# An attention encoder on one core: the count of branches in the dilated heads applied after the exponential

## The chip, the core and the metric

The kernel runs on one core of a Trainium2 chip. The metric is the device time of one execution in microseconds. An engine is named as the profile names it: PE is TensorE, DVE is VectorE, ACT is ScalarE, POOL is GpSimd, SP the queue that issues the DMAs.

## What is computed

Two sequences (a prompt of 1024 tokens and a sample of 512) go through two layers of width 1024. The first layer has 8 dilated heads ("a") and 8 latent heads ("b") side by side, the second 16 grouped-query heads ("c"). Each layer projects, attends, multiplies with a gate, projects back and normalises. Only the dilated heads matter here. Each is attention over three branches, (window 128, dilation 1), (512, 4), (2048, 16), whose denominators are merged:

```
for window, dilation in ((128, 1), (512, 4), (2048, 16)):      # one branch each
    s = q.k - slope * |t_query - t_key|     where the pair lies in the window and on the dilation, else -1e30
    m = max(s);  p = exp(s - m);  z = sum(p);  o = p.v
w = exp(m_branch - max over branches of m)
out = sum(o * w) / sum(z * w)
```

A pair of query and key may lie in one, two or three of the branches. It has the same score in each, so the result is one softmax in which the exponential of such a pair counts once, twice or three times.

## The kernel before

Everything is feature-major in SBUF; matmuls run on fp32r operands, and a product of better precision is made of parts: hi times hi and lo, and lo times hi.

The attention of a layer is one loop over `G` = heads x 10 tiles of keys (`NS` = 10 slots a head, s = g % 10). Even and odd tokens are kept apart (two "sides"). For a dilated head, slots 0 and 1 each hold two key tiles of the sample, slots 2 to 9 one key tile of the prompt (side 0, then side 1; tile m = 0 to 3). A key tile of 128 meets all 512 (sample: 256) queries of its own side and the 160 or 192 near ones of the other, so a tile is 832 columns wide in slots 0 and 1, 672 for m = 0 and 3, and 704 for m = 1 and 2.

Each engine walks the same slots in order and hands over by semaphores; nothing is planned at run time.

- PE, in slot g: `scores(g)`, then `pv(g - 3)` (LAG = 3), in which one or more `max_unit`s of head h + 1 stand between the part that needs the rounded probabilities and the part that needs their low part, then the remaining max units. `scores` writes the two banks SA, of which there is one copy: it waits for `e_done` of the slot before. The max units write the two halves of SM in turn: unit u waits until DVE is done with unit u - 2. Slots 0 to 3 have three units, slots 4 to 9 two; the heads of kinds b and c have two in each slot.
- `pair_scores` makes one tile for a dilated head out of seven matmuls: three parts for own-side columns (L1917 hi keys; L1918 identity x bias `Bhi`; L1921 low keys with the maximum subtracted), with L1920 adding the low part of the bias, `Blo`, over the 256 or 384 columns near the diagonal, and then three for the near columns of the other side (L1923, L1925, L1927).
- ACT, in slot g: waits for `s_ready`, exponential `PF` <- SA (L2185), then the rounded copy `PH` <- `PF` (L2188), except in slots 3 and 5 (`SLOW_HI`), where DVE makes it (L2380). After it, in slot 3, the inversion of the last head's denominators (`invert`, L2132 and L2134: logarithm and exponential), and in slot 5 that of its own sample.
- POOL, in slot g: the low part `PL` = `PF` - `PH` (L2486), except in slots 4 and 8 (`SLOW_LO`), where DVE makes it one slot later (L2301).
- DVE, in slot g, in this order: `augment` (slot 1, L2291), `normalise` of the last head (slot 4, L2333, waits for the inversion), the low part of slot g - 1 where it is DVE's, the rounded copy where it is DVE's, the first half of the maxima (L2264: adds the bias table to the scores in SM and takes the row maximum), `normalise` of the sample (slot 6), `bias_full` (slot 4), the other maxima, `augment` (slot 7), half of a bias table each in slots 7 and 8 (`bias`, L2245).

The bias of a pair is slope x distance plus the logarithm of the number of branches that hold it, -1e30 where none does. The table `Bhi` (1280 columns a head) is rounded to fp32r. `bias_full` (DVE, L2251) makes the same in full precision for 384 columns, and `bias_low` (POOL, L2468) the difference, `Blo`.

Of the kernel before, what the change touches and what calls it, by code (L numbers as in the profile page):

```python
# [25 lines left out]
BOWN, BCROSS, BLOW = 896, 192, 384  # L26
# [1415 lines left out]
def layer(nc, ar, l, tag, A, S, heads, gpost, ones, epst, xin, xout, sc, base, banks, place, project):  # L1442
# [86 lines left out]
    if NA:  # L1529
        b_hi, b_sum, b_lo = ar.sem(f"a_b_hi"), ar.sem(f"a_b_sum"), ar.sem(f"a_b_lo")  # L1530
# [52 lines left out]
    if NA:  # L1583
        sizes = (512, 4 * BW, 4 * BW, 32, 4 * BLOW, 4096, 4 * BW, 4 * BW, 4 * BLOW, 4 * BLOW)
        offsets = list(itertools.accumulate(sizes, initial=half1))
        BD, BL_ = (at(n, [P, BW], F32, offsets[1 + i]) for i, n in enumerate(("BD", "BL")))
        slope = at("slope", [P, 8], F32, offsets[3])
        BF = at("BF", [P, BLOW], F32, offsets[4])
        BS = at("BS", [P, 2 * CH], F32, offsets[5])
        Bhi = [at(f"Bhi{i}", [P, BW], F32R, (offsets[6], offsets[7], half0)[i]) for i in range(3)]  # L1590
        Blo = [at(f"Blo{i}", [P, BLOW], F32R, offsets[8 + i]) for i in range(2)]
# [283 lines left out]
    def tensor(pe, ahead):  # L1875
# [31 lines left out]
        def pair_scores(h, s, x, q1, q3, ka, kb):  # L1907
# [22 lines left out]
        def scores(h, s):  # L1930
# [193 lines left out]
    def scalar(act, ahead):  # L2124
# [55 lines left out]
        for g in range(G):  # L2180
# [5 lines left out]
            if s not in SLOW_HI:  # L2186
# [46 lines left out]
    def vector(dve, ahead):  # L2233
# [14 lines left out]
        def bias_full(h):  # L2248

            wait_count(dve, b_lo, h)  # L2250
            nc.vector.scalar_tensor_tensor(out=BF[:], in0=BD[:, 256:256 + BLOW],  # L2251
                                           scalar=slope[:, h:h + 1], in1=BL_[:, 256:256 + BLOW],
                                           op0=ALU.mult, op1=ALU.add).then_inc(b_sum, 1)
# [81 lines left out]
        def between(g, part):  # L2335
# [16 lines left out]
            if g == MAX0 and NA:  # L2352
                bias_full(0)
# [10 lines left out]
        for g in range(G):  # L2364
# [7 lines left out]
            if g > 0 and (g - 1) % NS in SLOW_LO:  # L2372
                low(g - 1)
# [4 lines left out]
            if s in SLOW_HI:  # L2378
# [6 lines left out]
            if s == 4 and h + 1 < NA:  # L2385
                bias_full(h + 1)
# [76 lines left out]
    def gpsimd(pool, ahead):  # L2463
        def bias_low(h):
            pool.wait_ge(b_hi, 2 * h + 2)
            pool.wait_ge(b_sum, h + 1)
            wait_count(pool, s_ready, NS * (h - 1))
            nc.gpsimd.tensor_tensor(Blo[h % 2][:], BF[:], Bhi[h % 3][:, 256:256 + BLOW].bitcast(F32), ALU.subtract  # L2468
                                    ).then_inc(b_lo, 1)

# [4 lines left out]
        def between(g):  # L2475
            if g == MAX0 and NA:
                bias_low(0)

        first.main.gpsimd(pool, between)
        for g in range(G):  # L2480
            h, s = g // NS, g % NS
            if s not in SLOW_LO:
# [7 lines left out]
            if s == 4 and h + 1 < NA:  # L2490
                bias_low(h + 1)
# [91 lines left out]
def shape_constants():  # L2583
# [26 lines left out]
    c["bias_count"] = np.where(held > 0, np.log(np.maximum(held, 1).astype(np.float64)), 0.0).astype(np.float32)  # L2610
# [51 lines left out]
```

## Time and profile before

| | us |
|---|---|
| median of 3 runs | 2054.36 (2050.83 to 2055.28) |
| the profiled execution | 2054.35 |
| its span, first to last instruction | 2052.6 |
| PE busy in the span | 2016.1 |
| DVE, ACT, POOL busy | 1211.8, 1129.9, 953.4 |
| the stage of the dilated heads | about 471 to 695 in the span |

A busy time is the sum of an engine's instructions, overlaps taken out. The ends of matmuls are modelled, so that a PE that is always busy in the profile needn't run at its best; starts are measured. The rows further down come from several views: the table of stages, the timeline (each instruction with its start and duration, in brackets the idle time before it and what ended it), one line of the code with all its instructions, and the chain that ended last.

### The profile page before, as it was taken

What the parts mean: (1) busy time and instruction counts of PE and PEld (TensorE: products, weight loads), DVE (VectorE), ACT (ScalarE), POOL (GpSimd) and SP (SyncE); (2) the same over time, 40 slices, a digit from 0 to 9 for tenths busy, and PEclk for the clock granted to TensorE, in tenths of its full rate; (3) what the DMA queues carried; (4) which work ended last, traced back from release to release, by engine and by line L of the source; (5) the groups of instructions that cost most, each with busy time, mean ns of one, the idle gap of its engine ahead of it and who ended that gap; (6) DMA issues with size and microseconds to landing.
All of it is one profiled execution on the core that took longest, in us unless ns stands there. A gap on an engine that the chain in (4) does not pass through costs nothing.

```text
span 2052.6 us, 25510 instructions
## 1 busy us (share of the span) xinstructions
PE 2016.1 (98%) x9456; PEld 1621.0 (79%) x9456; DVE 1211.8 (59%) x1941; ACT 1129.9 (55%) x1440; POOL 953.4 (46%) x487
## 2 busy tenths in 40 slices
PE   8999998999999999999999999999999999999998
PEld 6788886888888877777887777888777777777888
DVE  6632145325776666673559777414577778776454
ACT  6242234435666666665446444344677778888431
POOL 1222224435555555556102666433566676677401
PEclk9999998999999999999999999999999999999999
DMA  5133478617665754633435333362323343332534
GB/s 203 66 119 126 151 258 310 169 67 155 130 118 109 177 118 93 158 83 122 153 108 163 131 124 116 103 195 78 87 58 85 75 121 74 80 77 90 169 105 167
DMA packets 172143, 261.38 MB, mean 127 GB/s; under 512 B 78754, under 2 KB 89634, under 8 KB 172020
## 3 DMA queue, kind: packets, MB, share of 16 engines
q1 hardware_dynamic: 172020, 259.76, 44.6%
q8 instruction: 75, 1.23, 0.3%
q14 instruction: 48, 0.39, 0.1%
HBM read 161.78 MB, written 97.92 MB: 127 GB/s over the span
## 4 chain that ended last, share of the span: by engine, by line
PE 90%; ACT 3%; DVE 2%; DMA 2%; issue 1%; POOL 1%; SPq 0%; DVEq 0%; ACTq 0%
PE SA L1966 13%; PE OP L2012 11%; PE SM L1892 5%; PE SA L546 5%; PE OP L2019 5%; PE OP L546 5%; PE SM L2065 5%; PE OP L1104 4%; PE SA L2065 4%; PE SA L1104 4%; PE OS L2012 3%; PE OS L546 2%; PE OS L1104 2%; PE OS L2065 2%; PE SM L1888 2%; PE OS L2019 1%
## 5 line engine op out<-in xcount | busy, mean ns | idle before, releaser
L2486 POOL TENSOR_TENSOR c_PL<-c_PF,c_PH 128x1024 fp32r<-128x1024 f32 x128 | 307.7, 2407 | 137.6 <-ACT c_PH L2188 79.9
L2486 POOL TENSOR_TENSOR ab_PL<-ab_PF,ab_PH 128x1024 fp32r<-128x1024 f32 (+3 forms) x128 | 264.7, 2068 | 192.3 <-ACT ab_PH L2188 135.8
L2185 ACT ACTIVATE ab_PF<-SA 128x1024 f32<-128x1024 f32 (+3 forms) x160 | 143.7, 898 | 157.9 <-PE SA L1927 84.7
L2185 ACT ACTIVATE c_PF<-SA 128x1024 f32<-128x1024 f32 x160 | 164.6, 1029 | 84.4 <-PE SA L1966 83.0
L2273 DVE TENSOR_REDUCE c_MH<-SM 128x1 f32<-128x512 f32 x256 | 171.0, 684 | 66.4 <-PE SM L1892 66.3
L437 POOL TENSOR_TENSOR e_wl<-e_raw,e_wh 128x1024 fp32r<-128x1024 f32 (+1 forms) x30 | 70.6, 2354 | 185.1 <-ACT e_wh L613 185.1
L2188 ACT ACTIVATE c_PH<-c_PF 128x1024 fp32r<-128x1024 f32 x128 | 136.0, 1063 | 4.1
L1966 PE MATMUL SA<-c_Q,c_KA 128*128 128x512 f32 x320 | 127.8, 399 | 3.4 <-ACT c_PF L2185 3.4
L1966 PE MATMUL SA<-c_Q,c_KB 72*128 72x512 f32 x320 | 127.1, 397 | 0.0
L1036 POOL TENSOR_TENSOR n_wl<-n_raw,n_wh 128x1024 fp32r<-128x1024 f32 (+1 forms) x24 | 54.5, 2271 | 153.9 <-ACT n_wh L1201 153.9
L1892 PE MATMUL SM<-c_KA,c_Q 128*128 128x512 f32 x320 | 125.1, 392 | 0.0
L2188 ACT ACTIVATE ab_PH<-ab_PF 128x1024 fp32r<-128x1024 f32 (+3 forms) x128 | 119.8, 936 | 4.0
L2264 DVE CUSTOM_DVE_ANT_0 ab_BS<-SM,ab_Bhi 128x512 f32<-128x512 f32 (+1 forms) x192 | 85.9, 465 | 61.2 <-PE SM L1888 60.9
L2273 DVE TENSOR_REDUCE ab_MH<-SM 128x1 f32<-128x512 f32 x128 | 86.3, 687 | 47.0 <-PE SM L1892 45.1
L1966 PE MATMUL SA<-ab_Q,ab_KA 96*128 96x512 f32 x320 | 101.4, 398 | 0.2 <-ACT ab_PF L2185 0.2
L2012 PE MATMUL OP<-c_PH,c_VL 128*64 128x512 f32 x256 | 101.4, 396 | 0.0
L2012 PE MATMUL OP<-c_PH,c_VH 128*128 128x512 f32 x256 | 101.2, 395 | 0.0
L2012 PE MATMUL OP<-ab_PH,ab_VH 128*128 128x512 f32 (+2 forms) x256 | 92.6, 362 | 0.0
L2012 PE MATMUL OP<-ab_PH,ab_VL 128*64 128x512 f32 (+2 forms) x256 | 85.8, 356 | 0.0
L2019 PE MATMUL OP<-c_PL,c_VH 128*128 128x512 f32 x256 | 80.0, 394 | 0.0
L1892 PEld LDWEIGHTS SM<-c_KA,c_Q 128*128 128x128 f32 x320 | 60.2, 188 | 23.1 <-DVE c_MH L2273 0.2
L1966 PEld LDWEIGHTS SA<-c_Q,c_KA 128*128 128x128 f32 x320 | 60.5, 189 | 20.7 <-ACT c_PF L2185 5.5
(555 smaller groups left out, 5909.5 us busy)
## 6 DMA issues: line engine op xcount, KB each, us to landing
c_Q<-qC_hi SPq DMA_DIRECT2D x32, 384.0 KB, 5.0
e_raw<-in_w_tiles SPq DMA_DIRECT2D x20, 512.0 KB, 4.1
n_raw<-in_w_tiles SPq DMA_DIRECT2D x20, 512.0 KB, 3.7
e_XF<-in_xT SPq DMA_DIRECT2D x12, 512.0 KB, 10.6
silu_gate<-e_ta SPq DMA_DIRECT2D x24, 256.0 KB, 2.0
ab_Q<-qA_hi SPq DMA_DIRECT2D x16, 384.0 KB, 5.4
ab_G<-silu_gate SPq DMA_DIRECT2D x24, 256.0 KB, 3.7
ab_res<-in_xT SPq DMA_DIRECT2D x24, 256.0 KB, 2.9
```

The lines of the kernel that those rows point to most:

```text
L546: mm = nc.tensor.matmul(out, a[b][:, ks], x[:, k, cols(c)], start=(k + i == 0), stop=(k == KT - 1 and i == 2))
L1104: mm = nc.tensor.matmul(out, a[b][:, ks], x[c][k][:], start=(k + i == 0), stop=(k == KT - 1 and i == 2))
L1892: nc.tensor.matmul(SM[:, x * CH:(x + 1) * CH], Q1[h % 3][0:n, q0:q0 + P], keys(h)[0][0:n, k0:k0 + CH], start=True, stop=True).then_inc(m_r ...
L1966: mm = nc.tensor.matmul(out, w, y, start=(i == 0), stop=(i == len(mms) - 1))
L2012: nc.tensor.matmul(out[0:r], w[:, kt, :], PH[p][:, pc], start=(st and i == 0), stop=False, skip_group_check=h < NA)
L2019: mm = nc.tensor.matmul(out, vh[:, kt, :], PL[p][:, pc], start=False, stop=(en or h < NA), skip_group_check=h < NA)
L2065: mm = nc.tensor.matmul(acc[n % NB], w[t][:, ks], y, start=(k + i == 0), stop=(k == KT - 1 and i == 2))
L2185: nc.scalar.activation(used(PF[p], h, s), used(SA, h, s), ACT.Exp).then_inc(e_done, 1)
L2188: nc.scalar.activation(used(PH[p], h, s), used(PF[p], h, s), ACT.Copy).then_inc(p_hi[0], 1)
L2264: nc.vector.tensor_tensor_reduce(out=BS[:, x * CH:x * CH + n], in0=SM[:, x * CH:x * CH + n], in1=table.bitcast(F32), scale=1.0, scalar=-3. ...
L2273: nc.vector.reduce_max(dst, src, axis=AX_X).then_inc(m_done, 1)
L2486: nc.gpsimd.tensor_tensor(used(PL[p], h, s), used(PF[p], h, s), used(PH[p], h, s).bitcast(F32), ALU.subtract).then_inc(p_lo[0], 1)
```

## The change

- The bias loses the logarithm: `bias` becomes slope x distance, one `tensor_scalar` on DVE. `bias_full`, `bias_low`, their tables and L1920's matmuls go.
- A new table `held` (384 columns, values 1, 2 or 3) is loaded once. `counted(g)` on DVE multiplies the exponentials near the diagonal in place, 256 columns (m = 0 and 3, and each of a sample tile's two) or 384 (m = 1 and 2). It stands in DVE's slot g ahead of the maxima.
- ACT waits for it between the exponential and the rounded copy. In dilated heads ACT makes the copy in every slot, and POOL the low part in every slot; DVE makes neither.
- `pair_scores` alternates own-side and near columns, so that each pair of matmuls has the same weights.
- In slots of three max units, one stands right behind the scores, one inside `pv`, one behind it.

```diff
@@ counts
-            d = g % NS in on_dve
+            d = g % NS in on_dve and g >= NS * NA
@@ pair_scores
-            l0, l1 = max(0, P * m - P), min(n, P * m + 2 * P)
-            low = Blo[h % 2][:, l0 - P * m + P:l1 - P * m + P]
             nc.tensor.matmul(o, k1, side_of(q1, side, sample), start=True, stop=False, skip_group_check=True)
+            nc.tensor.matmul(c, k1, side_of(q1, 1 - side, sample)[:, v0:v1], start=not sample, stop=False,
+                             skip_group_check=True)
             nc.tensor.matmul(o, ident[:], own_bias(Bhi[h % 3], m, n), start=False, stop=False,
                              skip_group_check=True)
-            nc.tensor.matmul(o[:, l0:l1], ident[:], low, start=False, stop=False, skip_group_check=True)
+            nc.tensor.matmul(c, ident[:], cross_bias(Bhi[h % 3], side, m, v0, v1), start=False, stop=False,
+                             skip_group_check=True)
             nc.tensor.matmul(o, k3, side_of(q3, side, sample)[0:na, :], start=False, stop=True,
-                             skip_group_check=True)
-            nc.tensor.matmul(c, k1, side_of(q1, 1 - side, sample)[:, v0:v1], start=True, stop=False,
-                             skip_group_check=True)
-            nc.tensor.matmul(c, ident[:], cross_bias(Bhi[h % 3], side, m, v0, v1), start=False, stop=False,
                              skip_group_check=True)
@@ PE, first scores of a head
-                    pe.wait_ge(b_lo, h + 1)
+                    pe.wait_ge(b_hi, 2 * h + 2)
@@ PE, a slot
-            some = len(units) // 2
+            first_units, some = len(units) // 3, len(units) // 3 + len(units) // 2
             scores(h, s)
+            for u in units[:first_units]:
+                max_unit(h + 1, u)
             if g >= LAG:
-                pv(g - LAG, units[:some])
+                pv(g - LAG, units[first_units:some])
@@ ACT, a slot
-            if s not in SLOW_HI:
+            if s not in SLOW_HI or h < NA:
+                if h < NA:
+                    act.wait_ge(p_counted, g + 1)
                 act.wait_ge(e_done, g + 1)
                 nc.scalar.activation(used(PH[p], h, s), used(PF[p], h, s), ACT.Copy).then_inc(p_hi[0], 1)
@@ DVE
-            nc.vector.scalar_tensor_tensor(out=Bhi[h % 3][:, o], in0=BD[:, o], scalar=slope[:, h:h + 1],
-                                           in1=BL_[:, o], op0=ALU.mult, op1=ALU.add).then_inc(b_hi, 1)
+            nc.vector.tensor_scalar(Bhi[h % 3][:, o], BD[:, o], slope[:, h:h + 1], None, ALU.mult).then_inc(b_hi, 1)
+        def counted(g):
+            h, s = g // NS, g % NS
+            dve.wait_ge(e_done, g + 1)
+            for x in range(2 if s < 2 else 1):
+                _, m, sample = tile_of(s, x)
+                l0, l1 = max(0, P * m - P), min(256 if sample else CH, P * m + 2 * P)
+                p = PF[g % 4][:, x * CH + l0:x * CH + l1]
+                done = nc.vector.tensor_tensor(p, p, held[:, l0 - P * m + P:l1 - P * m + P], ALU.mult)
+            done.then_inc(p_counted, 1)
@@ DVE, a slot
-            if g > 0 and (g - 1) % NS in SLOW_LO:
+            if g > NS * NA and (g - 1) % NS in SLOW_LO:
                 low(g - 1)
...
-            if s in SLOW_HI:
+            if h < NA:
+                counted(g)
+            if s in SLOW_HI and h >= NA:
@@ POOL, a slot
-            if s not in SLOW_LO:
+            if s not in SLOW_LO or h < NA:
```

## Rows read from the trace of the kernel before

**Rows 1.** The page, busy time of each engine, share of the span, instructions.
```profile
PE 2016.1 (98%) x9456; PEld 1621.0 (79%) x9456; DVE 1211.8 (59%) x1941; ACT 1129.9 (55%) x1440; POOL 953.4 (46%) x487
```

**Rows 2.** Table of stages: stretch, length, busy us of each engine, clock, DMA.
```profile
560.00:590.00 30.00, 29.79 (x194) 26.00 (x193) 21.44 (x67) 19.00 (x24) 15.31 (x11) 1.00 0.66 134
```

**Rows 3.** The chain that ended last, one matmul five heads apart: start us, us.
```profile
507.36 0.50 PE SM L1888
...
648.21 0.50 PE SM L1888
```

**Rows 4.** PE timeline, a prompt tile's scores: start us, us, instruction.
```profile
564.03 0.40 PE L1917 MATMUL SA<-ab_Q,ab_KA 128*128 128x512 f32 x1
...
564.49 0.33 PE L1920 MATMUL SA<-ab_Blo,ab_ident 128*128 128x384 f32 x1
564.66 0.40 PE L1921 MATMUL SA<-ab_Q,ab_KB 72*128 72x512 f32 x1
564.90 0.26 PE L1923 MATMUL SA<-ab_Q,ab_KA 128*128 128x192 f32 x1
564.99 0.28 PE L1925 MATMUL SA<-ab_Bhi,ab_ident 128*128 128x192 f32 x1
565.10 0.27 PE L1927 MATMUL SA<-ab_Q,ab_KB 72*128 72x192 f32 x1
```

**Rows 5.** One line of code each, heads 1 to 6: ns least/median/most, starts, forms.
```profile
L2185 ACT ACTIVATE ab_PF<-SA x60: 732/760/869, 499.9 to 666.0; 128x672 f32<-128x672 f32 x24, 128x704 f32<-128x704 f32 x24, 128x832 f32<-128x832 f32 x12
L2188 ACT ACTIVATE ab_PH<-ab_PF x48: 765/793/903, 500.8 to 666.8; 128x672 fp32r<-128x672 f32 x18, 128x704 fp32r<-128x704 f32 x18, 128x832 fp32r<-128x832 f32 x12
L2486 POOL TENSOR_TENSOR ab_PL<-ab_PF,ab_PH x47: 1627/1701/1988, 501.8 to 662.7; 128x672 fp32r<-128x672 f32 x23, 128x832 fp32r<-128x832 f32 x12, 128x704 fp32r<-128x704 f32 x12
```

**Rows 6.** Timeline of POOL and DVE, low parts beside POOL and alone.
```profile
514.75 1.01 POOL L2468 TENSOR_TENSOR ab_Blo<-ab_BF,ab_Bhi 128x384 fp32r<-128x384 f32 x1 [2.57 <-issue]
...
514.82 1.70 DVE L2301 TENSOR_TENSOR ab_PL<-ab_PF,ab_PH 128x704 fp32r<-128x704 f32 x1
...
525.80 0.88 DVE L2301 TENSOR_TENSOR ab_PL<-ab_PF,ab_PH 128x704 fp32r<-128x704 f32 x1
...
711.66 1.22 DVE L2301 TENSOR_TENSOR ab_PL<-ab_PF,ab_PH 128x1024 fp32r<-128x1024 f32 x1
```

**Rows 7.** The same view of three DVE lines.
```profile
L2245 DVE SCALAR_TENSOR_TENSOR ab_Bhi<-ab_BD,ab_slope,ab_BL x10: 873/1142/1424, 522.8 to 637.7; 128x640 fp32r<-128x640 f32 x10
...
L2264 DVE CUSTOM_DVE_ANT_0 ab_BS<-SM,ab_Bhi x143: 304/424/694, 500.8 to 666.9; 128x512 f32<-128x512 f32 x48, 128x160 f32<-128x160 f32 x47, 128x256 f32<-128x256 f32 x24, 128x192 f32<-128x192 f32 x24
...
L2291 DVE TENSOR_TENSOR ab_Q<-MT,ab_negsel x12: 681/949/1217, 502.1 to 662.9; 8x1024 fp32r<-8x1024 f32 x6, 8x512 fp32r<-8x512 f32 x6
```

**Rows 8.** Timeline of ACT and POOL, from copy to low part.
```profile
563.15 0.77 ACT L2188 ACTIVATE ab_PH<-ab_PF 128x672 fp32r<-128x672 f32 x1
...
563.99 1.63 POOL L2486 TENSOR_TENSOR ab_PL<-ab_PF,ab_PH 128x672 fp32r<-128x672 f32 x1 [0.44 <-ACT ab_PH L2188]
```

**Rows 9.** Timeline, a maximum on DVE and PE's weight load that waits for it.
```profile
563.20 0.42 DVE L2264 CUSTOM_DVE_ANT_0 ab_BS<-SM,ab_Bhi 128x256 f32<-128x256 f32 x1 [1.56 <-PE SM L1888]
...
563.69 0.19 PEld L1888 LDWEIGHTS SM<-ab_KA,ab_Q 128*128 128x128 f32 x1 [0.26 <-DVE ab_MS L2264]
```

**Rows 10.** Timeline of ACT and DVE in slot 3, head 3.
```profile
565.41 0.76 ACT L2185 ACTIVATE ab_PF<-SA 128x704 f32<-128x704 f32 x1 [1.49 <-PE SA L1927]
...
566.19 1.02 ACT L2132 ACTIVATE ab_RZ<-OP 64x1024 f32<-64x1024 f32 x1
...
568.35 1.22 DVE L2333 TENSOR_TENSOR ab_OB<-OP,ab_RZ 64x1024 f32<-64x1024 f32 x1 [0.22 <-ACT ab_RZ L2134]
```

**Rows 11.** Timeline of PE, first and last score matmul of a sample tile.
```profile
501.53 0.33 PE L1917 MATMUL SA<-ab_Q,ab_KA 128*128 128x256 f32 x1
...
503.05 0.28 PE L1927 MATMUL SA<-ab_Q,ab_KB 72*128 72x160 f32 x1
```

**Rows 12.** One line, second step of the inversions, both sizes.
```profile
L2134 ACT ACTIVATE ab_RZ<-ab_RZ x12: 632/848/1068, 510.9 to 657.3; 64x1024 f32<-64x1024 f32 x6, 64x512 f32<-64x512 f32 x6
```

More of the change, by code:

```diff
@@ L25 @@
 ROPE = 32
-BOWN, BCROSS, BLOW = 896, 192, 384
+BOWN, BCROSS, COUNTED = 896, 192, 384
 BW = BOWN + 2 * BCROSS
@@ L1529, in layer @@
     if NA:
-        b_hi, b_sum, b_lo = ar.sem(f"a_b_hi"), ar.sem(f"a_b_sum"), ar.sem(f"a_b_lo")
+        b_hi, p_counted = ar.sem(f"a_b_hi"), ar.sem(f"a_p_counted")
     SA, SM, OP, OS, MT = banks
@@ L1583, in layer @@
     if NA:
-        sizes = (512, 4 * BW, 4 * BW, 32, 4 * BLOW, 4096, 4 * BW, 4 * BW, 4 * BLOW, 4 * BLOW)
+        sizes = (512, 4 * BW, 32, 4 * COUNTED, 4096, 4 * BW, 4 * BW)
         offsets = list(itertools.accumulate(sizes, initial=half1))
[L1586 to L1591, printed above, removed]
+        BD = at("BD", [P, BW], F32, offsets[1])
+        slope = at("slope", [P, 8], F32, offsets[2])
+        held = at("held", [P, COUNTED], F32, offsets[3])
+        BS = at("BS", [P, 2 * CH], F32, offsets[4])
+        Bhi = [at(f"Bhi{i}", [P, BW], F32R, (offsets[5], offsets[6], half0)[i]) for i in range(3)]
     MAX0 = 7
@@ L1659, in load_constants @@
             for dst, src in [(ident_in[:], A["ident"]), (negsel[:], A["negsel"])] + (
-                    [(BD[:], A["bias_dist"]), (BL_[:], A["bias_count"]), (slope[:], A["slopes"])] if NA else []):
+                    [(BD[:], A["bias_dist"]), (held[:], A["held"]), (slope[:], A["slopes"])] if NA else []):
                 sp.dma_start(dst, src).then_inc(const_in, 16)
@@ L2033, in tensor @@
             units = units_of(h + 1, s) if h + 1 < NH else ()
-            some = len(units) // 2
+            first_units, some = len(units) // 3, len(units) // 3 + len(units) // 2
             scores(h, s)
+            for u in units[:first_units]:
+                max_unit(h + 1, u)
             if g >= LAG:
-                pv(g - LAG, units[:some])
+                pv(g - LAG, units[first_units:some])
             else:
-                for u in units[:some]:
+                for u in units[first_units:some]:
                     max_unit(h + 1, u)
@@ L2244, in bias @@
             o = slice(half * BW // 2, (half + 1) * BW // 2)
-            nc.vector.scalar_tensor_tensor(out=Bhi[h % 3][:, o], in0=BD[:, o], scalar=slope[:, h:h + 1],
-                                           in1=BL_[:, o], op0=ALU.mult, op1=ALU.add).then_inc(b_hi, 1)
[L2248 to L2253, printed above, removed]
+            nc.vector.tensor_scalar(Bhi[h % 3][:, o], BD[:, o], slope[:, h:h + 1], None, ALU.mult).then_inc(b_hi, 1)
[8 more added lines that the diff above has]
+            done.then_inc(p_counted, 1)
         def maximum(h, u):
@@ L2351, in between @@
                 set_ones(0, const_set, 1)
-            if g == MAX0 and NA:
-                bias_full(0)
             if g in (MAX0 + 1, MAX0 + 2) and NA:
@@ L2384, in vector @@
                 normalise(h, 0)
-            if s == 4 and h + 1 < NA:
-                bias_full(h + 1)
             for u in units[some:]:
@@ L2463, in gpsimd @@
     def gpsimd(pool, ahead):
[L2464 to L2469, printed above, removed]
         def low_weights(t):
@@ L2473, in low_weights @@
             nc.gpsimd.tensor_tensor(WL[t][:], WF[t][:], WH[t][:].bitcast(F32), ALU.subtract).then_inc(w_lo, 1)
[L2475 to L2479, printed above, removed]
+        first.main.gpsimd(pool, lambda g: None)
         for g in range(G):
             h, s = g // NS, g % NS
-            if s not in SLOW_LO:
+            if s not in SLOW_LO or h < NA:
                 on, n = hi_at[g]
@@ L2489, in gpsimd @@
                 first.last_gated(pool)
-            if s == 4 and h + 1 < NA:
-                bias_low(h + 1)
             if (h, s) in ((LAST, 4), (LAST, 8)):
@@ L2609, in shape_constants @@
     c["bias_dist"] = np.where(held > 0, -off.astype(np.float64), -1e30).astype(np.float32)
-    c["bias_count"] = np.where(held > 0, np.log(np.maximum(held, 1).astype(np.float64)), 0.0).astype(np.float32)
+    c["held"] = np.maximum(held, 1)[:, 384 - P:384 - P + COUNTED].astype(np.float32)
     c["slopes"] = np.ascontiguousarray(np.broadcast_to(2.0 ** -np.arange(1, 9, dtype=np.float32), (P, 8)))
```

## The prediction

> **What bounds the kernel now.** I read the page's table of engines first: TensorE is busy 98% of the span [rows 1]. The change touches only the eight dilated heads, so next comes the table of stages: in thirty microseconds in the middle of them PE is busy 29.79, DVE 21.44, ACT 19.00, POOL 15.31 at full granted clock [rows 2]. The chain of work passes the same matmul of head after head, 140.85 us apart over five heads [rows 3]: 28.17 us a head, ten score tiles each ("slots" s0 to s9; s0 and s1 are the sample's, two blocks in one tile). PE sets this beat. ACT is idle for a third of it, and all that the change does to ACT has to fit in there. But idle time on average says nothing of a serial chain; that is the question here.
>
> **What PE is spared.** L1920, the low part of the bias, goes: 12 matmuls a head, 8 of 256 columns and 4 of 384. Matmul ends are modelled, so I price by starts: 384 columns cost 564.49 to 564.66, 0.17 us [rows 4]; 256 columns in proportion 0.115. A head: 8 x 0.115 + 4 x 0.17 = 1.60 us, eight heads 12.8 us. Order: the three short products c stand in a row now, starts 564.90, 564.99, 565.10 [rows 4]; 192 columns stream in 0.08, and the later ones wait 0.11 for weights. Between long ones each load hides behind a 512-column matmul; I take 0.03 us a product, some 0.08 a prompt tile, 64 tiles: 5 us. (Bounds 0 and 8.) In sample tiles all are short, no gain. Sum for PE: 18 us; its beat would be 28.17 - 1.60 - 0.64 = 25.9 us.
>
> **What the chain gains in length.** Now a tile goes exp (L2185, ACT), then at once the rounded copy (L2188, ACT), then the low part (L2486, POOL). After the change ACT waits between exp and copy for DVE's multiplication (counted), in order, so the next tile's exp and with it PE's scores after that (the SA banks are single: scores(g+1) waits for e_done) are queued behind it. And in all ten slots ACT makes the copy and POOL the low part; DVE made two of each. Sizes: exp 0.73, 0.76, 0.87 us for 672, 704, 832 columns; copy 0.77, 0.79, 0.90; POOL 1.63, 1.70, 1.98 [rows 5]. The new multiplication has the form of L2301, a tensor_tensor with two SBUF inputs: 0.88 for 704 columns, 1.22 for 1024, both alone [rows 6], so 1.06 ns a column and 0.13 fixed: 0.41 for 256 columns (slots 2, 5, 6, 9), 0.54 for 384 (3, 4, 7, 8), 0.75 for the two of a sample tile. Bounds for it: as for 704 columns 0.88; and POOL's own tensor_tensor of 384, 1.01 [rows 6], is the dearest neighbour; I take the line through DVE's own rows.
>
> **POOL in its way.** The same L2301 takes 1.70 us where POOL began a tensor_tensor 0.07 before it: it ends at 516.52, 0.76 after POOL's end at 515.76 [rows 6], so it hardly moved while POOL ran and saved 0.12 of its 0.88. L2245 shows it too, 873 ns at least and 1424 at most [rows 7]. The maxima (one input from PSUM) go on beside POOL. After the change counted(g) always comes in this window: POOL starts the low part of g-1 0.07 after the copy of g-1 (563.92 to 563.99 [rows 8]), just as ACT starts exp of g, and runs 1.63 to 1.98 against exp's 0.73 to 0.87. So counted(g) ends at the earliest at POOL's end + its own time - 0.12. The Trainium skill, "SBUF — State Buffer", section "SBUF: two separate sides", says that the pair shared by VectorE and GpSimd is an exclusive lock, held for the whole instruction by whoever starts first. By the letter the 0.12 would not be saved, some 6 slots x 8 heads x 0.12 = 6 us more, 2107 in place of 2101; the row shows the smaller figure and the sum uses it.
>
> **A second new loop.** With three units in slots 0 to 3, PE's third max unit u2 may start only when DVE is done with u0 (two halves of SM). PE now issues u0 right behind the scores, but DVE takes counted(g) first. So counted(g), max u0, u2, scores(g+1), exp(g+1), counted(g+1) is a ring. A 256-column max frees PE 0.49 after its start [rows 9]; at present that costs PE idle 0.26 [rows 9].
>
> **One head, from the end C of one counted to the next.** Handovers 0.05 where no row tells; exp starts 0.31 after the start of the last score matmul (565.10 to 565.41 [rows 4, 10]). Copy ends at C + 0.82 (672), 0.84 (704), 0.95 (sample).
> - s9 to s0: 0.82 + 0.07 + 1.63 POOL + 0.75 - 0.12 = 3.15
> - s0 to s1, ring: 0.49 max + 0.18 u2 + scores 1.29 (501.53 to 503.05 is 1.52 [rows 11], less 2 x 0.115) + 0.31 + 0.87 + 0.04 + 0.75 = 3.93
> - s1 to s2: POOL's 1.98: 0.95 + 0.07 + 1.98 + 0.29 = 3.29
> - s2 to s3, ring: 0.49 + 0.30 (u2 of 512) + scores 0.87 (1.07 [rows 4] less 0.17 and some of the 0.08) + 0.31 + 0.76 + 0.04 + 0.54 = 3.31
> - s3 to s4: copy 0.84, then the inversion for the last head, 2.16 (566.19 to 568.35), on ACT; its end frees DVE's normalisation, 1.22 [rows 10], which stands ahead of counted(4): 0.84 + 2.16 + 1.22 + 0.54 = 4.76. Before, no copy on ACT here and nobody waited for DVE.
> - s4 to s5: 0.84 + 0.07 + 1.70 + 0.29 = 2.90
> - s5 to s6: 0.82 + sample inversion 2 x 0.63 [rows 12] + 0.02 + 0.73 + 0.04 + 0.41 = 3.28 (POOL is done by then)
> - s6 to s7: 0.82 + 0.07 + 1.63 + 0.42 = 2.94
> - s7 to s8 and s8 to s9: DVE has two maxima (up to 0.69 [rows 7]), in s7 an augment of 0.68 [rows 7], and half a bias table before the next counted. The table gets cheaper (one input; between half and all of 0.87 [rows 7], I take 0.47), but it too starts while POOL runs and ends some 0.33 behind it, then counted: 0.84 + 0.07 + 1.70 + 0.33 + 0.50 = 3.44, and 3.30.
>
> Sum 34.3 us a head against 28.17: +6.1. PE needs 25.9 of it and would stand idle a quarter. Heads 0 to 5: +6.1 each (head 0 has no inversion in slot 3 but the last gate's sigmoid); head 6 has no bias work, +5.3; head 7's maxima are the other kind, two a slot, so no ring, +4.7. In all 36.8 + 5.3 + 4.7 = 47 us. PE's 18 us are inside that and not to be subtracted again. The profiled execution took 2054.35 us (span 2052.6 and 1.75 around it), the median of the runs 2054.36; so 2054.35 + 47 = **2101 us**.
>
> At nothing: the constant table that is no longer loaded and one that is (the projection lies over both), bias_full and bias_low (DVE and POOL idle time beside PE; were the cover gone, 1.01 a head on POOL [rows 6]), the other two kinds of head, whose counts and order stay, and a maximum without the logarithm (values change, no instruction). POOL has 17.3 us of low parts a head and a lag of three slots before PE wants them: not late.
>
> **Rivals.**
> 1. POOL doesn't hold counted up (so short an operation passes). Then the POOL steps shrink: 2.5, 3.93, 2.9, 3.31, 4.76, 2.1, 3.28, then PE's beat 2.3, 2.6, 2.3: 30.0 a head, +1.9 for seven, about 0 for the last: 13 us, **2067**. Against: every L2301 and L2245 that meets POOL is stretched. For: none of the rows has so short an operation.
> 2. Faster: the new wait is covered. ACT's chain alone, with neither POOL nor the ring, is exp 7.7 + copies 8.0 + inversions 3.4 + counted 5.3 + normalise 1.2 + handovers 1.1 = 26.7 us a head. The place is ACT between exp and copy; the point from which it decides is a head's chain of 28.17. At 26.7 the gain is 8 x 1.5 = 12 us, **2042**; if PE stayed the bound at 25.9, 2036. It needs both stalls absent; for it speaks only that ACT is idle 11 of 30 us [rows 2].
> 3. Dearer: counted gets nothing done at all beside POOL (6 of 10 slots x 8 x 0.12, +6) and 0.1 more at each of 80 handovers (+8): **2115**.
>
> **How the numbers follow.** Forecast 0.72 (own range 2088 to 2114), rival 1 0.13, rival 2 0.08, rival 3 and beyond 0.04, no change by gains and stalls in balance 0.03. The range for 8 in 10 takes in rival 1 and nearly all of the forecast: 2064 to 2114. Faster by over 0.2% (what a measurement of this kernel tells from none): 0.08; within 0.2%: 0.03; slower: 0.89.
>
> **What would show it.** In the profile after: no L1920; the stage of dilated heads 34 us a head and PE with idle time whose releaser is ACT's exp; ACT idle between exp and copy with DVE as releaser, about 1.2 us in most slots; multiplications of 256 columns that last over 1 us when POOL runs and 0.4 when not; a gap of 4.8 us between the counted of slots 3 and 4; the b and c heads as before. Wrong would be: multiplications at 0.4 to 0.55 throughout (rival 1), or a head at 26 to 27 us with PE still without gaps (rival 2).

## The result, and the profile after

The changed kernel takes 2101.15 us (median of 4 runs, 2099.3 to 2103.35) against 2053.48 of the kernel before beside it: a ratio of 1.0232, 95% interval 1.0219 to 1.0244. The profiled execution took 2101.11 us, its span is 2099.3. The forecast was 2101.

The page, engines (answers to [rows 1]):

```profile
PE 2020.2 (96%) x9360; PEld 1618.3 (77%) x9360; DVE 1246.1 (59%) x1997; ACT 1136.9 (54%) x1456; POOL 973.6 (46%) x495
```

There are 96 matmuls fewer, yet PE's busy time is 4 us more: the ends of matmuls are modelled, so busy time is no measure of what PE was spared. The span is what grew. The stretch of the dilated heads, from the first exponential of the first head to the first exponential after the eighth, is 472.30 to 697.05 before and 470.27 to 741.83 after: 224.75 and 271.56 us, 46.8 more, which is all of the 46.7 between the spans. What stands ahead of it is 2.0 us shorter, what follows 1.9 longer (1355.6 and 1357.5).

The table of stages (stretch, length, busy us of PE, PEld, DVE, ACT, POOL with counts, granted clock, DMA share, GB/s); the middle row answers to [rows 2]:

```profile
470.00:500.00 30.00, 23.44 (x128) 20.21 (x126) 16.20 (x54) 16.32 (x22) 13.96 (x9) 0.83 0.36 84
560.00:590.00 30.00, 24.31 (x152) 20.13 (x151) 21.25 (x63) 16.55 (x22) 16.00 (x10) 1.00 0.52 110
620.00:680.00 60.00, 51.27 (x302) 42.86 (x302) 43.74 (x120) 33.84 (x44) 30.26 (x19) 0.94 0.45 98
```

PE falls from 29.79 to 24.31 of 30 us while no other engine is near full: a serial chain, not a busy engine, sets the beat. The granted clock is 1.00 (2.4 GHz) in the middle; the 0.83 and 0.94 of the two others are means over time at 2.4 and at 1.2 GHz.

The waits of four heads of after, 540 to 676 us (engine, line, what it waited for: total, times, longest):

```profile
ACT ab_PH L2188 <- DVE ab_PF L2255: 46.1, 41, 2.0
...
PEld SM L1887 <- DVE ab_MS L2267: 14.7, 12, 1.6
...
PEld SA L1914 <- ACT ab_PF L2183: 8.5, 8, 1.5
```

L2188 is the rounded copy, L2255 counted, L1887 a max unit, L1914 the first score matmul. Every tile's copy waits for the multiplication, 46.1 us in four heads, 11.5 a head, 1.12 a copy. PE waits 14.7 us for a free half of SM (the second loop of the prediction) and 8.5 for the exponentials.

Two steps of one head, slots 3 to 5 of head 3, ACT and DVE (start, duration, instruction, idle before it and what ended it):

```profile
586.89 0.79 ACT L2188 ACTIVATE ab_PH<-ab_PF 128x704 fp32r<-128x704 f32 x1 [0.62 <-DVE ab_PF L2255]
...
587.71 1.02 ACT L2130 ACTIVATE ab_RZ<-OP 64x1024 f32<-64x1024 f32 x1
...
588.76 1.06 ACT L2132 ACTIVATE ab_RZ<-ab_RZ 64x1024 f32<-64x1024 f32 x1
...
589.86 1.22 DVE L2336 TENSOR_TENSOR ab_OB<-OP,ab_RZ 64x1024 f32<-64x1024 f32 x1 [1.87 <-ACT ab_RZ L2132]
...
591.00 0.54 DVE L2255 TENSOR_TENSOR ab_PF<-ab_PF,ab_held 128x384 f32<-128x384 f32 x1
...
591.57 0.79 ACT L2188 ACTIVATE ab_PH<-ab_PF 128x704 fp32r<-128x704 f32 x1 [0.97 <-DVE ab_PF L2255]
...
594.46 0.77 ACT L2188 ACTIVATE ab_PH<-ab_PF 128x672 fp32r<-128x672 f32 x1 [1.48 <-DVE ab_PF L2255]
```

From copy to copy this is 4.68 and 2.89 us; the prediction had 4.76 and 2.90. L2130 and L2132 are the inversion, L2336 the normalisation, both ahead of the multiplication at 591.00.

DVE and POOL beside one another in the same head:

```profile
592.44 1.70 POOL L2476 TENSOR_TENSOR ab_PL<-ab_PF,ab_PH 128x704 fp32r<-128x704 f32 x1 [2.97 <-ACT ab_PH L2188]
...
593.01 1.41 DVE L2255 TENSOR_TENSOR ab_PF<-ab_PF,ab_held 128x256 f32<-128x256 f32 x1 [0.59 <-ACT ab_PF L2183]
...
597.29 0.43 DVE L2255 TENSOR_TENSOR ab_PF<-ab_PF,ab_held 128x256 f32<-128x256 f32 x1 [2.01 <-ACT ab_PF L2183]
...
598.59 1.64 POOL L2476 TENSOR_TENSOR ab_PL<-ab_PF,ab_PH 128x672 fp32r<-128x672 f32 x1 [1.69 <-ACT ab_PH L2188]
...
599.41 1.24 DVE L2255 TENSOR_TENSOR ab_PF<-ab_PF,ab_held 128x384 f32<-128x384 f32 x1 [0.25 <-ACT ab_PF L2183]
...
604.88 0.54 DVE L2245 TENSOR_SCALAR ab_Bhi<-ab_BD,ab_slope 128x640 fp32r<-128x640 f32 x1
604.97 2.00 POOL L2476 TENSOR_TENSOR ab_PL<-ab_PF,ab_PH 128x704 fp32r<-128x704 f32 x1 [1.72 <-ACT ab_PH L2188]
...
605.55 1.71 DVE L2255 TENSOR_TENSOR ab_PF<-ab_PF,ab_held 128x256 f32<-128x256 f32 x1
```

counted at 593.01 began 0.57 behind POOL, took 1.41 and ended at 594.42, 0.28 after POOL's end at 594.14. The one at 597.29 met no POOL: 0.43. The one at 599.41 (384 columns) ended 0.42 after POOL's. At 604.88 the bias table began 0.09 ahead of POOL: it took 0.54, and POOL's low part took 2.00 in place of 1.70. The counted behind that ran 1.71 and ended 0.29 after POOL. All multiplications from 530 to 700 us, one line (ns least/median/most, starts, forms):

```profile
L2255 DVE TENSOR_TENSOR ab_PF<-ab_PF,ab_held x60: 410/552/1711, 531.4 to 699.3; 128x256 f32<-128x256 f32 x40, 128x384 f32<-128x384 f32 x20
```

The second loop, head 4, slot 1, with PE's weight load for the third max unit:

```profile
613.55 0.76 DVE L2255 TENSOR_TENSOR ab_PF<-ab_PF,ab_held 128x256 f32<-128x256 f32 x2 [0.67 <-ACT ab_PF L2183]
...
614.61 0.19 PEld L1887 LDWEIGHTS SM<-ab_KA,ab_Q 128*128 128x128 f32 x1 [1.03 <-DVE ab_MS L2267]
```

counted (two pieces, 0.76) is followed by the maxima, and PE's load had waited 1.03 us for the one that began at 614.23 and the accumulator read behind it.

### The profile page after: what moved, and what is told of

Same layout as the page of the kernel before. It is cut to its first block, busy times and chain, and to the rows that moved or that the text cites. A ratio compares the mean times of both kernels' runs of the same rounds, so it can differ in the third digit from the quotient of the medians.

```text
span 2099.3 us, 25469 instructions
## 1 busy us (share of the span) xinstructions
PE 2020.2 (96%) x9360; PEld 1618.3 (77%) x9360; DVE 1246.1 (59%) x1997; ACT 1136.9 (54%) x1456; POOL 973.6 (46%) x495
## 4 chain that ended last, share of the span: by engine, by line
PE 82%; DVE 6%; ACT 6%; issue 3%; DMA 1%; POOL 1%; SPq 0%; DVEq 0%; ACTq 0%
PE SA L1962 12%; PE OP L2008 9%; PE SA L546 5%; PE SM L1891 5%; PE OP L546 5%; PE OP L1104 5%; PE SA L1104 4%; PE SM L2063 4%; PE OP L2015 4%; PE SA L2063 4%; DVE ab_PF L2255 3%; PE OS L546 2%; PE OS L1104 2%; ACT ab_PF L2183 2%; PE OS L2008 2%
## 5 line engine op out<-in xcount | busy, mean ns | idle before, releaser
L2476 POOL TENSOR_TENSOR ab_PL<-ab_PF,ab_PH 128x1024 fp32r<-128x1024 f32 (+3 forms) x144 | 293.3, 2037 | 233.5 <-ACT ab_PH L2188 198.5
L2188 ACT ACTIVATE ab_PH<-ab_PF 128x1024 fp32r<-128x1024 f32 (+3 forms) x144 | 132.0, 917 | 95.1 <-DVE ab_PF L2255 93.1
L2188 ACT ACTIVATE c_PH<-c_PF 128x1024 fp32r<-128x1024 f32 x128 | 135.7, 1060 | 4.1
L2255 DVE TENSOR_TENSOR ab_PF<-ab_PF,ab_held 128x256 f32<-128x256 f32 (+1 forms) x96 | 76.5, 810 | 56.1 <-ACT ab_PF L2183 55.4
L1887 PE MATMUL SM<-ab_KA,ab_Q 128*128 128x512 f32 (+1 forms) x192 | 67.4, 354 | 29.8 <-DVE ab_MS L2267 21.8
```

What stands on the lines that cost most here:

```text
L2188: nc.scalar.activation(used(PH[p], h, s), used(PF[p], h, s), ACT.Copy).then_inc(p_hi[0], 1)
L2255: done = nc.vector.tensor_tensor(p, p, held[:, l0 - P * m + P:l1 - P * m + P], ALU.mult)
L2476: nc.gpsimd.tensor_tensor(used(PL[p], h, s), used(PF[p], h, s), used(PH[p], h, s).bitcast(F32), ALU.subtract).then_inc(p_lo[0], 1)
```

## Experiments

The theory: (a) counted(g) is locked out by POOL's low part of tile g - 1; (b) ACT's wait for it, in order, delays the next exponential; (c) the ring over the maxima; PE's savings lie under these. The rivals: the multiplications cost what they cost, whatever POOL does; or one of the edits on PE is what hurts. "Head" is the distance between the first exponentials of neighbouring heads in the middle of the stage: 28.17 before, 34.00 after. "Head 0" is the same distance for the first head, which has more around it: 27.65 before, 35.67 after.

**e1: POOL's low part of 64 columns instead of the whole tile** (after; PE reads the rounded tile in its place, so the low part of the probabilities is left out). Same waits, same instructions, only POOL's duration differs.

```diff
-                mm = nc.tensor.matmul(out, vh[:, kt, :], PL[p][:, pc], start=False,
+                mm = nc.tensor.matmul(out, vh[:, kt, :], (PH if h < NA else PL)[p][:, pc], start=False,
-                nc.gpsimd.tensor_tensor(used(PL[p], h, s), used(PF[p], h, s), used(PH[p], h, s).bitcast(F32),
+                few = (lambda t: t[:, 0:64]) if h < NA else (lambda t: t[:])
+                nc.gpsimd.tensor_tensor(few(PL[p]), few(PF[p]), few(PH[p]).bitcast(F32),
```

> The changed kernel, but POOL's low part in the dilated heads covers 64 columns of each tile in place of 672 to 832, and PE's low product reads PH in its place (left out: the low part of the probabilities, so the result of the dilated heads isn't the reference's). The count, its wait and PE's work are unchanged. Theory: POOL's tensor_tensor holds the multiplication up in most slots; without it a head takes 30.0 us instead of 34.0, the time falls by about 30 us to 2070, and every multiplication lasts 0.4 to 0.55 us. Rival (the cost is the wait in ACT's order alone, POOL is harmless): no change, 2101 within 4.

Measured: 2068.56 us, ratio 1.008 [1.0065, 1.0095], head 30.00. Its multiplications and its row of the table of stages:

```profile
L2255 DVE TENSOR_TENSOR ab_PF<-ab_PF,ab_held x54: 418/426/561, 538.6 to 674.7; 128x256 f32<-128x256 f32 x36, 128x384 f32<-128x384 f32 x18
...
560.00:590.00 30.00, 26.86 (x172) 22.71 (x171) 19.81 (x70) 18.83 (x24) 3.55 (x10) 1.00 0.55 119
```

No multiplication is above 561 ns (after: 1711), and the head is 30.00, the very figure of the prediction's rival 1. The sum fits better than its steps: copy to copy, s9 to s0 takes 3.18 where rival 1 had 2.5, and s8 to s9 1.91 where it had 2.3. So POOL's share of the price is 4.0 us a head, 32.6 us in all; but 16 us over the kernel before are left with POOL out of the way (5.7 of them in head 0, 33.38), and PE is still at 26.86 of 30.

**e3: no counted and no wait for it** (after; the count of branches is left out).

```diff
-                if h < NA:
-                    act.wait_ge(p_counted, g + 1)
@@ DVE, a slot
-            if h < NA:
-                counted(g)
```

> The changed kernel without the multiplication and without ACT's wait for it (left out: the count of branches in the dilated heads). All else as changed: ten copies a head on ACT, ten low parts on POOL, six matmuls a tile in alternating order. Theory: the whole loss hangs on the multiplication between exponential and copy; without it PE is the bound again at 25.9 us a head, some 18 us under the kernel before: 2036, with PE busy 99% in the stage. Rival (the two more copies on ACT and low parts on POOL cost by themselves): 2045 or more, with PE waiting for exponentials behind the inversions.

Measured: 2038.7 us, ratio 0.9936 [0.9919, 0.9953], head 25.95. PE full again:

```profile
560.00:590.00 30.00, 29.82 (x198) 26.12 (x197) 19.18 (x61) 22.48 (x29) 19.37 (x12) 1.00 0.73 143
```

All else in the change is worth a gain of 14 us; the multiplication with its waits costs 62. The copies and low parts of all ten slots on ACT and POOL are in this kernel too, and PE hardly waits: what was given to those engines is no cause.

**e6: ACT makes the copy of tile g - 1 behind the exponential of tile g** (after). The wait stays, but nothing is queued behind it that PE needs soon, and POOL's low part starts later, when counted(g) has mostly run.

```diff
@@ ACT
             nc.scalar.activation(used(PF[p], h, s), used(SA, h, s), ACT.Exp).then_inc(e_done, 1)
-            if s not in SLOW_HI or h < NA:
-                if h < NA:
-                    act.wait_ge(p_counted, g + 1)
+            if 0 < g <= NS * NA:
+                copy_counted(g - 1)      # waits for p_counted, g
+            if s not in SLOW_HI and h >= NA:
```

> The changed kernel, whole result, with one step moved: ACT makes the rounded copy of tile g-1 behind the exponential of tile g (in the dilated heads), so the multiplication runs while ACT waits for PE or computes the next exponential, and it starts before POOL's low part of the tile before. Theory: the chain through ACT and POOL is open, and what is left over PE's 25.9 us is the ring over the maxima in slots 0 to 3 (about 1.4 us a head) and the inversion in slot 3 (0.3): 27.6 us a head, 2050 us. Rival (the lag of three tiles is used up by the later copy, and PE then waits for the copy in front of its second product): above 2060, with PE's wait for ACT's copy in the trace.

Measured: 2065.3 us, ratio 1.0062 [1.0047, 1.0077], head 28.42: a miss by 15 us. ACT's exponentials over slots 0 to 3 of head 3, start and duration:

```profile
566.12 0.86 ACT L2188 ACTIVATE ab_PF<-SA 128x832 f32<-128x832 f32 x1 [1.30 <-PE SA L1923]
...
570.04 0.86 ACT L2188 ACTIVATE ab_PF<-SA 128x832 f32<-128x832 f32 x1 [2.41 <-PE SA L1923]
...
573.40 0.73 ACT L2188 ACTIVATE ab_PF<-SA 128x672 f32<-128x672 f32 x1 [1.71 <-PE SA L1923]
...
576.54 0.76 ACT L2188 ACTIVATE ab_PF<-SA 128x704 f32<-128x704 f32 x1 [1.62 <-PE SA L1923]
```

3.92, 3.36, 3.14 us apart, each with ACT idle and waiting for scores. In e1, with POOL out of the way, the same three are 3.93, 3.36, 3.13: the later copy leaves them as they are. The prediction named the ring in two of these steps and POOL in the middle one; the ring holds all three. It is dearer than I had set it (1.4 us a head), and it is what is late next once (a) and (b) are gone.

But the ring makes only 0.8 of a head of the miss (28.42 for 27.6), some 6 us. The rest is head 0, which takes 38.26. There, the granted clock is 0.50, which is 1.2 GHz, from 474 to 484 us, and the chain runs over a load that is issued 8.3 us later than in e7 (488.14, shown further down), because the SP queue stores the last gate first (493.04), and POOL makes that gate's product (491.76) behind a low part:

```profile
496.45 8.28 DMA ab_Q<-qA_lo
```

**e7: e6, and in slots of three units DVE takes the first maximum ahead of counted.**

```diff
@@ DVE, a slot
+            early = 1 if h < NA and len(units) == 3 else 0
+            for u in units[:early]:
+                maximum(h + 1, u)
             if h < NA:
                 counted(g)
-            for u in units[:some]:
+            for u in units[early:some]:
                 maximum(h + 1, u)
```

> As the run with the later copy, whole result, and DVE takes the first of three maxima of a slot ahead of the multiplication (slots 0 to 3). Theory: this opens the second ring too: 26.0 to 26.4 us a head, 2037 to 2041 us, faster than both kernels. Rival (the ring over the maxima isn't what holds slots 0 to 3): the same time as the run with the later copy alone.

Measured: **2041.4 us**, ratio 0.9947 [0.9932, 0.9962], head 25.77. It leaves nothing out of the computation, and is faster than both kernels. The same four exponentials, all multiplications of the middle heads, and the table of stages:

```profile
580.13 0.86 ACT L2188 ACTIVATE ab_PF<-SA 128x832 f32<-128x832 f32 x1 [1.30 <-PE SA L1923]
...
582.98 0.86 ACT L2188 ACTIVATE ab_PF<-SA 128x832 f32<-128x832 f32 x1 [1.32 <-PE SA L1923]
...
585.45 0.73 ACT L2188 ACTIVATE ab_PF<-SA 128x672 f32<-128x672 f32 x1 [0.82 <-PE SA L1923]
...
587.95 0.76 ACT L2188 ACTIVATE ab_PF<-SA 128x704 f32<-128x704 f32 x1 [0.98 <-PE SA L1923]
...
L2260 DVE TENSOR_TENSOR ab_PF<-ab_PF,ab_held x63: 411/540/805, 541.1 to 674.6; 128x256 f32<-128x256 f32 x42, 128x384 f32<-128x384 f32 x21
...
560.00:590.00 30.00, 30.00 (x203) 26.58 (x202) 24.63 (x82) 21.15 (x29) 20.93 (x13) 1.00 0.74 146
```

2.85, 2.47, 2.50 apart in place of e6's 3.92, 3.36, 3.14, so 10.42 becomes 7.82: 2.6 us a head for three maxima in another place (heads 1 to 6 give 14.5 of the 24 us between e6 and e7, head 0 6.5, 38.26 to 31.72). PE is busy 30.00 of 30. The multiplication is still on DVE, and still up to 805 ns long, and costs a middle head nothing: no copy of ACT waits for it any more in 530 to 680 us.

**e2: the first maximum ahead of counted, alone** (the edit of e7 on after, copy where after has it).

> The changed kernel, whole result, but in slots of three maxima DVE takes the first ahead of the multiplication. Theory (the ring counted, max u0, u2, scores, exp sets slots 1 and 3): these two steps fall to what ACT and POOL need, 3.93 to 3.62 and 3.28 to 2.94 us, 0.65 us a head for seven heads, 4 to 5 us in all: 2096 to 2097, and a head of 33.4 us. Rival (the ring is only a symptom of late exponentials): within 1 us of 2101.

Measured: 2093.91 us, ratio 1.0197 [1.0183, 1.0211], head 33.33. The steps that were the ring's fall from 3.93 to 3.59 and from 3.28 to 2.93; s1 to s2, which POOL sets, stays at 3.28. With ACT's order in place the ring gives back only 0.67 a head, for the other loop is right behind it. The time is 2 us below the forecast, because head 0 falls further, 35.67 to 33.19: the third and fourth exponentials there come 3.50 and 3.12 behind the ones before them, and in after, where PE ran at 1.2 GHz, 4.42 and 4.29.

**e8: the normalisation behind counted in slot 4** (after).

```diff
@@ DVE, a slot
-            if s == 4 and h > 0:
-                normalise(h - 1, 1)
...
                 counted(g)
+            if s == 4 and h > 0:
+                normalise(h - 1, 1)
```

> The changed kernel, whole result, with DVE's normalisation of the last head in slot 4 moved behind the multiplication. Theory: the step from slot 3 to slot 4 loses the wait for it, from 4.68 to 0.84 + 2.13 + 0.76 + 0.04 + 0.54 = 4.31, some 0.4 us a head for seven heads, 3 us: 2098. Rival (the later normalisation delays the maxima and is paid one slot on): within 1 us of 2101.

Measured: 2101.38 us, ratio 1.0232 [1.0218, 1.0246], head 33.67. Head 3, the copies of slots 3 and 4:

```profile
588.49 0.79 ACT L2188 ACTIVATE ab_PH<-ab_PF 128x704 fp32r<-128x704 f32 x1 [0.63 <-DVE ab_PF L2255]
...
592.83 0.79 ACT L2188 ACTIVATE ab_PH<-ab_PF 128x704 fp32r<-128x704 f32 x1 [0.63 <-DVE ab_PF L2255]
```

Copy to copy 4.34 in place of 4.68: the exponential stands behind the inversion on ACT, so of the 1.22 of normalisation only 0.34 was to be had. The step came as expected, and the head is 0.33 shorter, but the time isn't: it is where the rival had it, though not by the rival's way, since no other step of such a head got longer. Heads 1 and 4 of this profile take 35.48 and 35.33, and in both the granted clock is at the lower level for a few us:

```profile
511.00:514.00 3.00, 3.00 (x14) 2.70 (x14) 1.09 (x4) 0.86 (x1) 0.77 (x1) 0.50 1.06 229
...
613.00:616.00 3.00, 3.00 (x15) 2.80 (x14) 1.30 (x3) 0.65 (x1) 1.61 (x1) 0.50 1.00 213
```

In after no middle head is that long. These two heads lose some 3.5 us, more than the edit gains. Of the four runs, the two with a mean granted clock of 0.986 took 2103.15 and 2104.52 us, the two at 0.989 and 0.991 took 2099.61 and 2098.31. So the gain is probably there and covered by the clock; whether the edit itself brings the lower clock about isn't shown.

Four kernels price PE's side, made from the kernel before.

**e5: before, without L1920's matmuls** (the tables are still made; the low part of the bias is left out).

> The kernel before without the 96 matmuls of the bias's low part (left out: that low part; its table is still made by DVE and POOL). Theory: PE sets the beat, and 1.60 us a head goes: 12.8 us less, 2040. Rival (part of it is covered because PE then waits for maxima or exponentials): 8 us or less.

Measured: 2042.07 us, ratio 0.9944 [0.993, 0.9958], head 26.57: 28.17 less 1.60, the prediction's figure to the last digit. The time fell by 11 us, not 12.8: in head 0 (27.65 to 27.13) and head 7 (28.08 to 26.69) less was to be had.

**e4: before, score matmuls in alternating order, nothing else.**

> The kernel before with the alternating order of the score matmuls alone, low part of the bias kept (whole result). Theory: in prompt tiles each short matmul stands between long ones and its weight load is covered, 0.08 us a tile, 64 tiles: 5 us less (bounds 0 and 8), 2048. Rival (the matmuls' pace doesn't depend on order): no change.

Measured: 2052.86 us, ratio 1.0001 [0.9993, 1.001], head 28.15. A miss: nothing. The same tile as [rows 4]:

```profile
563.70 0.40 PE L1917 MATMUL SA<-ab_Q,ab_KA 128*128 128x512 f32 x1
563.93 0.25 PE L1918 MATMUL SA<-ab_Q,ab_KA 128*128 128x192 f32 x1
564.02 0.42 PE L1920 MATMUL SA<-ab_Bhi,ab_ident 128*128 128x512 f32 x1
564.27 0.34 PE L1922 MATMUL SA<-ab_Blo,ab_ident 128*128 128x384 f32 x1
...
564.88 0.30 PE L2012 MATMUL OS<-ab_PH,ab_VH 128*128 128x256 f32 x1
```

The first score matmul to the first of what follows is 1.18 us, and in before 564.03 to 565.21, the same. A short product costs 0.09 here against 0.09 to 0.11, but the 512-column matmuls behind one take 0.25 against 0.23.

**e10: before, with the new places of the max units on PE.**

```diff
@@ PE, a slot
-            some = len(units) // 2
+            first_units, some = len(units) // 3, len(units) // 3 + len(units) // 2
             scores(h, s)
+            for u in units[:first_units]:
+                max_unit(h + 1, u)
             if g >= LAG:
-                pv(g - LAG, units[:some])
+                pv(g - LAG, units[first_units:some])
```

> The kernel before with the new places of the three max units alone (whole result): one behind the scores, one inside the second product, one behind it. The run with the alternating order alone moved nothing, yet PE's beat where nothing holds it is 25.8 to 25.95 us, 0.6 to 0.8 less than 28.17 less the 1.60 of the low part. Theory: these 0.6 to 0.8 us are waits of PE for maxima that this order removes (0.26 and 0.22 stand in the trace of before in slots 0 to 3), 4 to 5 us in all: 2048. Rival (they come from the pair of both orders, or from DVE's lighter slots): 1 us or less.

Measured: 2049.76 us, ratio 0.9978 [0.9969, 0.9987], head 27.30. The waits of before between 500 and 667 us, on the halves of SM:

```profile
PEld SM L1888 <- DVE ab_MS L2264: 3.1, 12, 0.3
PEld SM L1888 <- DVE ab_MH L2264: 1.4, 6, 0.2
```

and the only one left in e10:

```profile
PEld SM L1888 <- DVE ab_MH L2266: 1.0, 6, 0.2
```

4.5 us in six heads fall to 1.0, 0.58 a head. The edit is worth 0.87 a head, so only part of it is a wait that the profile names.

**e11: e5 and e10 together.**

> The kernel before without the low part's matmuls (left out: the low part of the bias) and with the new places of the max units. Theory: the two add up, 26.57 less 0.7 us a head: 25.9 us a head and 2037 us, about what the run without the count reached (2038.7). Rival (they overlap, since a shorter tile also changes which maximum PE waits for): 2041 or more.

Measured: 2036.23 us, ratio 0.9918 [0.9905, 0.9932], head 25.76. 28.17 - 1.60 - 0.87 = 25.70: the two add up to within 0.06, and reach the head of e7 (25.77), 0.19 below that of e3. PE's beat is settled without the alternation.

**e9: e7, with the last gate's sigmoid two slots earlier on ACT and its product three on POOL.** What is left over in e7 is head 0, 31.7 us. There, PE waits for a load, in the chain and in PE's timeline:

```profile
488.14 8.36 DMA ab_Q<-qA_lo
...
498.56 0.55 PE L1914 MATMUL SA<-ab_Q,ab_KA 128*128 128x256 f32 x1 [2.85 <-issue]
```

```diff
@@ ACT
-            if g == 3:
+            if g == 1:
                 first.last_sigmoid(act)
@@ POOL
-            if g == 3:
+            if g == 0:
                 first.last_gated(pool)
```

> As the run with the later copy and the first maximum ahead (2041.4), whole result, and the last gate of the projection is finished early: its sigmoid in slot 1 in place of 3, its product on POOL after slot 0 in place of 3. The SP queue stores that gate before it loads the low operands of the second head, for which PE stood in the first head (31.7 us in place of 25.8). Theory: the load is issued some 6 us earlier and 4 to 5 us go: 2036 to 2038. Rival (the loads wait for something else, or the sigmoid delays the exponentials of slots 2 and 3 by as much): no change.

Measured: 2047.97 us, ratio 0.9976 [0.9965, 0.9986], slower than e7 by 6.6. A miss. The first load is issued at 478.82 in place of 485.10, and head 0 is 30.18 in place of 31.72, but head 1 is 31.0 in place of 27.17. From the chain that ended last, what holds it now:

```profile
492.05 1.34 DVE ab_KB L2241
...
496.30 1.32 DVE ab_Bhi L2250
...
507.12 2.43 DVE ab_PF L2260 x2
```

DVE: ones written into a key buffer (L2241), a bias table (L2250) and multiplications of up to 1.2 us a piece, with maxima between them, almost without a gap. In the profiled executions, which lie 8.5 us apart, the eight heads take 2.2 us more than in e7, what stands ahead of them 1.2, and what follows them, the same code, 5.1 more. I can't say why, so most of the loss stays open.

## Why the prediction was right, step by step

- **The chain, not PE, sets the beat: right.** Copy to copy, eight of the ten steps of a head are within 0.03 us of their forecast: 3.12, 3.93, 3.27, 3.28, 4.68, 2.89, 3.29, 2.93, 3.42, 3.19 for s9 to s0 onward, against 3.15, 3.93, 3.29, 3.31, 4.76, 2.90, 3.28, 2.94, 3.44, 3.30. The two others are off by 0.08 and 0.11. The sum is 34.0 in place of 34.3. Two figures came out nearly right by another way than forecast: the sample tile's 0.75 (measured 0.76) isn't on the prediction's own line, which gives 2 x 0.41 = 0.82; and in s8 to s9 the bias table didn't wait for POOL but began ahead of it and made POOL 0.30 longer (rows at 604.88).
- **POOL locks counted out: right, and rival 1 falls.** e1 shows both: with POOL short, a median of 426 ns and a head of 30.00. By the rows above, a multiplication ends at POOL's end plus its own time less 0.12 to 0.15, as the row of the kernel before had it (0.12). The Trainium skill, "SBUF — State Buffer", section "SBUF: two separate sides", says that the one who starts second fully blocks; on the length of the wait and on who wins (604.88: DVE first, and POOL is the one that is stretched) the trace agrees, on the last 0.12 us it doesn't.
- **The ring: right in after, under-rated as what comes next.** Its two steps were forecast to 0.03. The step between them, given to POOL, is held by the ring as well (e1: exponentials 3.36 apart without POOL). But rival 2 lists what a head takes with "neither POOL nor the ring" in one, and I expected e6 to be near PE's beat; the ring held e6 at 28.42 a head. It costs 2.6 us a head between e6 and e7.
- **What would show it: all but one line.** No L1920, 34 us a head, copies that wait 1.1 us for DVE (46.1 over 41; forecast about 1.2), multiplications over 1 us beside POOL, the gap between slots 3 and 4. But PE's idle time was to have ACT's exponential as releaser, and of the 23.2 us that the two rows name only 8.5 have; 14.7 end with a maximum, which is late because it stands behind counted. That row pointed at the ring before e6 did.
- **Normalisation in slot 4: right** (4.68 for 4.76; e8 moved it as worked out). Heads 6 and 7 came at 33.31 and 32.60, 5.1 and 4.4 over 28.17, where 5.3 and 4.7 were forecast.
- **Head 0 was mis-sized:** forecast +6.1, measured +8.0 (27.65 to 35.67). 0.5 of the 1.9 between them is that head 0 of before takes 27.65 and not 28.17. Three steps are longer than in later heads, by 2.7 us together, of which the first exponential gives part back (it stands 3.82 ahead of the second, in later heads 4.69). From 476 to 485 us the granted clock is 0.50, so PE is at 1.2 GHz, after a stretch (470 to 476) in which it was busy 2.45 of 6 us. A prompt tile's 512-column products then start 0.65 apart, short one included, against 0.33 in head 3 (580.78 to 581.11). Two rows of PE's timeline, one of the table of stages and one of DVE's timeline:

```profile
476.34 0.71 PE L1914 MATMUL SA<-ab_Q,ab_KA 128*128 128x512 f32 x1
...
476.99 0.71 PE L1917 MATMUL SA<-ab_Bhi,ab_ident 128*128 128x512 f32 x1
...
476.00:485.00 9.00, 7.76 (x27) 6.79 (x28) 3.25 (x15) 3.75 (x6) 3.57 (x2) 0.50 0.01 2
...
496.70 1.34 DVE L2236 MEMSET ab_KB<- 64x1536 f32 x1 [0.38 <-issue]
```

These scores are part of the ring, and its steps s1 to s2 and s2 to s3 are 3.95 and 4.45 in head 0, copy to copy, against 3.27 and 3.28 later: 1.85 more. And DVE writes the ones of a key buffer, 1.34 us, ahead of the multiplication of slot 7: s6 to s7 takes 3.75 in place of 2.93. The prediction has neither term. In e2 the granted clock is 0.95 in 473 to 480, and the first two of these steps are as in its later heads. The 1.9 us missing here offset the 0.3 a head too much that the forecast had in heads 1 to 5, so that the sum, 47 against 46.8, looks better than its parts.
- **PE's beat: the total nearly right, one term wrong.** 25.9 was forecast, 25.76 to 25.95 measured. The low part's 1.60 is exact (e5). The 0.64 a head that the prediction gave to alternation is 0.02 (e4). I took the 0.11 between starts of short products for weights that can be hidden; in turn with long ones, the time comes back on the long one. In its place stands the edit that I gave no gain at all, the places of the max units: 0.87 (e10). Two errors of opposite sign, so that the total is luck; neither reached the forecast of the time, since PE isn't the bound there.
- **At nothing: right.** e3, with the full load of copies and low parts, runs within 0.2 of PE's beat (25.95 against e11's 25.76).
- **The rule that decides the other side:** rival 2's ACT chain was put at 26.7 a head. e7 lies below that, at 25.77, since in it ACT asks for a tile that is already counted: the chain of 26.7 had 5.3 us of counted in it.

## What to carry to other kernels

A step that is cheap where it is counted (0.41 us of DVE) costs its wait once it is put into a handover between in-order engines: ask what stands behind the waiting instruction, and let it wait one tile later, behind the work that others need. Look at whether the new instruction meets one of another engine that holds it up: here a tensor_tensor of POOL started just ahead of it in most slots, and it got POOL's duration, not its own. And when a loop is cut, name the next-longest one before promising the gain; here, with the copy's order alone (e6), the kernel was still 12 us slower than the kernel before, and with three maxima a head moved too (e7) some 12 us faster.

## What the runs showed of the chip that I had not expected

- Interleaving short and long fp32r matmuls doesn't make them cheaper: 1.18 us a tile in either order (e4).
- Three max units spread among other work, in place of two of them in a row, gave PE 0.87 us a head, of which the waits in the profile name 0.58; the other 0.29 stays open.
- The hold-up between DVE and POOL works in both directions, and a short instruction holds a long one up: a table of 0.54 us on DVE that began 0.09 ahead made POOL's low part 0.30 longer (2.00 for 1.70).
- With PE's gaps came a lower clock, but not everywhere: the granted clock is 0.83 in 470 to 500 and 0.94 in 620 to 680 of after, and 1.00 in 560 to 590, where PE has gaps too. Before has 1.00 in 470 to 500. It costs what the chain loses by slower matmuls: 1.85 us in the two ring steps of head 0, some 3.5 us in heads 1 and 4 of e8, and nothing to be seen in 620 to 680, where the heads take 34.00 and 33.96.
